# The product of p with its projection computed in the embedding norm's stage, and the gates' two column halves interleaved with a lag of three tiles

## The reference

```python
h = layer_norm(x, ln_emb_g, ln_emb_b)                 # first step of the second block
...
h = layer_norm(DEEPNORM_ALPHA * h + out, ln1_g[i], ln1_b[i])
gate = jax.nn.sigmoid(jnp.einsum('bld,de->ble', h, w_ple_gate[i]))   # 1024 x 1024 weights
ple = jnp.einsum('blq,qd->bld', p[i], w_ple_proj[i])                 # 256 x 1024 weights
h = layer_norm(DEEPNORM_ALPHA * h + gate * ple, ln2_g[i], ln2_b[i])
```

## Time and profile before

| | |
|---|---|
| median of 3 timed runs | 2349.52 us (2346.97 to 2352.33) |
| the profiled execution's own time | 2353.53 us |
| its span in the trace | 2351.8 us |
| TensorE (PE) busy | 2130.5 us, 91% of the span |
| TensorE weight loads (PEld) busy | 1665.2 us, 71% |
| VectorE (DVE) busy | 1750.1 us, 74% |
| ScalarE (ACT) busy | 1057.5 us, 45% |
| GpSimd (POOL) busy | 181.9 us, 8% |
| mean granted TensorE clock | 0.94 |

### The profile page before, as it was taken

The page is one execution under the profiler, slowest core; times in us unless marked ns, Lnnn a source line. Parts: engine busy times, 40 slices in busy tenths (PEclk is TensorE's granted clock), DMA queues, the critical chain, the costliest instruction groups (busy, mean ns, idle before and its releaser), DMA issues. The chain is left out here.

```text
span 2351.8 us, 25583 instructions
## 1 busy us (share of the span) xinstructions
PE 2130.5 (91%) x10156; PEld 1665.2 (71%) x10156; DVE 1750.1 (74%) x1852; ACT 1057.5 (45%) x1194; POOL 181.9 (8%) x154
## 2 busy tenths in 40 slices
PE   5999988999946999999999289999999959899997
PEld 3767835668825888888887168888887647788775
DVE  4575158995575999999997649999999458954727
ACT  4387135773315777777775122221221346622123
POOL 2000010000000111111110200000000010141210
PEclk8999997999967999999999589999999968899999
DMA  9111170002286999999997501212222130332201
GB/s 322 45 36 36 36 283 1 1 1 82 114 315 241 335 395 402 394 394 402 393 394 246 163 13 63 82 36 72 72 99 81 63 117 1 126 116 90 72 1 72
DMA packets 123456, 365.03 MB, mean 155 GB/s; under 512 B 10035, under 2 KB 20683, under 8 KB 123360
## 3 DMA queue, kind: packets, MB, share of 16 engines
q1 hardware_dynamic: 110560, 326.84, 36.4%
q0 software_dynamic: 7568, 23.09, 4.0%
q10 hardware_dynamic: 5232, 13.78, 1.5%
HBM read 324.76 MB, written 38.86 MB: 155 GB/s over the span
## 5 line engine op out<-in xcount | busy, mean ns | idle before, releaser
L2121 DVE SCALAR_TENSOR_TENSOR arena<-arena,vecs 128x1023 f32<-128x1023 f32 (+14 forms) x240 | 304.4, 1268 | 7.1
L1639 DVE TENSOR_TENSOR w_low<-W,w_high 128x2048 fp32r<-128x2048 f32 x96 | 217.0, 2287 | 39.1 <-ACT w_high L1591 39.1
L2018 PE MATMUL Q<-hT_high,w_high 128*128 128x512 f32 (+1 forms) x736 | 227.2, 392 | 5.9 <-DVE ring_low L2164 5.8
L1639 DVE TENSOR_TENSOR w_low<-arena,w_high 128x2048 fp32r<-128x2048 f32 x96 | 218.4, 2290 | 17.7 <-ACT w_high L1591 17.7
L1591 ACT ACTIVATE w_high<-W 128x2048 fp32r<-128x2048 f32 x96 | 184.0, 1919 | 97.0 <-PE Q L1534 65.4
L2018 PE MATMUL Q<-hT_low,w_high 128*128 128x512 f32 (+1 forms) x720 | 222.7, 391 | 0.0
L1591 ACT ACTIVATE w_high<-arena 128x2048 fp32r<-128x2048 f32 x96 | 184.2, 1919 | 74.9 <-PE Q L1534 74.9
L2018 PE MATMUL Q<-hT_high,ring_low 128*128 128x512 f32 x704 | 217.2, 390 | 0.0
L2018 PEld LDWEIGHTS Q<-hT_high,w_high 128*128 128x128 f32 (+1 forms) x736 | 135.5, 184 | 38.9 <-DVE ring_low L2164 5.9
L1534 PE MATMUL Q<-w_high,x_high 128*128 128x512 f32 x512 | 160.8, 396 | 2.4 <-DVE x_low L1642 2.4
L1534 PE MATMUL Q<-w_low,x_high 128*128 128x512 f32 x512 | 158.9, 392 | 0.0
(11 more groups left out here) (450 smaller groups left out, 4304.0 us busy)
## 6 DMA issues: line engine op xcount, KB each, us to landing
W<-in_w_dram SPq DMA_DIRECT2D x48, 2048.0 KB, 12.3
arena<-in_w_dram SPq DMA_DIRECT2D x48, 2048.0 KB, 11.3
W<-in_w_mod_dram SPq DMA_DIRECT2D x12, 2048.0 KB, 13.4
W<-in_w_in_dram SPq DMA_DIRECT2D x12, 2048.0 KB, 8.5
W<-in_w_out_dram SPq DMA_DIRECT2D x6, 2048.0 KB, 11.5
spill<-arena ACTq DMA_DIRECT2D x24, 512.0 KB, 2.6
W<-in_w_in_dram SPq DMA_DIRECT2D x8, 1024.0 KB, 7.2
arena<-in_x_dram SPq DMA_DIRECT2D x4, 1024.0 KB, 17.4
```

The source lines that it names most:

```text
L1639: nc.vector.tensor_tensor(wl[:], chunk_src(r, j), wh[:].bitcast(F32), ALU.subtract).then_inc(low_v, 1)
L2018: ins = nc.tensor.matmul(Q[rows, 2 * (n % 4) + half, :], w[:, k], x[:, k, HALF * half:HALF * half + HALF], start=k == 0 and w is high and ...
L2121: ins = nc.vector.scalar_tensor_tensor(conf[:, i, j:], u[:, 0:S - j], w, conf[:, i, j:], ALU.mult, ALU.add)
```

## The change

The product of p with its projection leaves the tail. In the stage of the embedding norm ScalarE's queue now also loads p and w_ple_proj, TensorE turns p and computes the 16 products (2 before tile 0's transposes, then 2 behind each tile's), ScalarE copies each out of PSUM (`keep_ple`) and stores it to a new DRAM tensor `ple_rows`. In the tail SyncE loads these rows back into `arena`, and VectorE multiplies from there. The gates run in a new order `g_order`: first-half tile q, then second-half tile q - 3.

```diff
+        ple_stage = tiles(12, PLE_SLOTS, HALF)
...
                 act.dma_start(emb_b, bc_row(A["ln_emb_b_2"], D)).then_inc(vec_in, 16)
+                act.dma_start(p_sb, A["p_2"][0, 0].rearrange("(t p) q -> p t q", p=P)).then_inc(p_in, 16)
+                act.dma_start(w_ple, A["w_ple_proj_2"][0].rearrange("(k p) n -> p k n", p=P)).then_inc(w_ple_in, 16)
...
+                def keep_ple(i):
+                    t, n = divmod(i, 2)
+                    j = i % PLE_SLOTS
+                    act.wait_ge(ple_mm, i + 1)
+                    if i >= PLE_SLOTS:
+                        act.wait_ge(ple_stored[j], 16)
+                    nc.scalar.activation(ple_stage[:, j], Q[:, 6 + i % 2, :], ACT.Copy).then_inc(ple_kept, 1)
+                    act.wait_ge(ple_kept, i + 1)
+                    act.dma_start(ple_rows[P * t:P * t + P, HALF * n:HALF * n + HALF], ple_stage[:, j])\
+                        .then_inc(ple_stored[j], 16)
+
                 root(0)
+                act.wait_ge(p_tr, 1)
+                for j in range(2):
+                    nc.scalar.activation(pT[:, j], bank2(2 + j), ACT.Copy).then_inc(pT_ready, 1)
                 for t in range(NT):
                     if t + 1 < NT:
                         root(t + 1)
...
+                    for i in (2 * t, 2 * t + 1):
+                        keep_ple(i)
+                for j in range(PLE_SLOTS):
+                    act.wait_ge(ple_stored[j], 16 * (2 * NT // PLE_SLOTS))
 
             @block.tensor
             def _(pe):
+                def ple(i):
+                    t, n = divmod(i, 2)
+                    if i >= 2:
+                        pe.wait_ge(ple_kept, i - 1)
+                    for k in range(2):
+                        ins = nc.tensor.matmul(Q[:, 6 + i % 2, :], pT[:, k, P * t:P * t + P],
+                                               w_ple[:, k, HALF * n:HALF * n + HALF], start=k == 0, stop=k == 1)
+                    ins.then_inc(ple_mm, 1)
+
+                pe.wait_ge(p_in, 16)
+                for j in range(2):
+                    for t in range(NT):
+                        ins = nc.tensor.transpose(Q[:, 4 + 2 * j + t // 4, P * (t % 4):P * (t % 4) + P],
+                                                  p_sb[:, t, P * j:P * j + P], ident[:])
+                ins.then_inc(p_tr, 1)
+                pe.wait_ge(w_ple_in, 16)
+                pe.wait_ge(pT_ready, 2)
+                ple(0)
+                ple(1)
                 for t in range(NT):
                     pe.wait_ge(emb_ready, t + 1)
...
                     ins.then_inc(emb_tr, 1)
+                    if t + 1 < NT:
+                        ple(2 * t + 2)
+                        ple(2 * t + 3)
...
+        GATE_LAG = 3
+        g_order = [(n, t) for q in range(NT + GATE_LAG) for n, t in ((0, q), (1, q - GATE_LAG)) if 0 <= t < NT]
...
-                sync.dma_start(p_sb, A["p_2"][0, 0].rearrange("(t p) q -> p t q", p=P)).then_inc(p_in, 16)
-                sync.dma_start(w_ple, A["w_ple_proj_2"][0].rearrange("(k p) n -> p k n", p=P)).then_inc(tail_in, 16)
+                sync.dma_start(tiles(8, NT, HALF), ple_of[:, :, 0:HALF]).then_inc(ple_in[0], 16)
+                sync.dma_start(tiles(12, 4, HALF), ple_of[:, 0:4, HALF:]).then_inc(ple_in[1], 16)
...
+                sync.wait_ge(ple_read, g_order.index((0, 3)) + 1)
+                sync.dma_start(tiles(8, 4, HALF), ple_of[:, 4:NT, HALF:]).then_inc(ple_in[2], 16)
...
-                for i in range(2 * NT):
-                    if i == 2:
-                        act.wait_ge(p_tr, 1)
-                        for j in range(2):
-                            nc.scalar.activation(pT[:, j], bank2(j), ACT.Copy).then_inc(pT_ready, 1)
-                    if i == NT // 2:
+                for i, (n, t) in enumerate(g_order):
+                    if (n, t) == (0, 1):
                         unit_high_part(5)
...
-                    if i > NT:
-                        root_2(act, i - NT - 1)
+                    if n == 1 and t:
+                        root_2(act, t - 1)
...
-                        nc.vector.tensor_tensor(g, g, Q[:, i % 4, :], ALU.mult).then_inc(ple_mult, 1)
+                    nc.vector.tensor_tensor(g, g, ple_at[NT * n + t], ALU.mult).then_inc(ple_mult, 1)
```

More of the change, by code:

```diff
@@ L63, in program @@
     cs_rows = dram("cs_rows", (P, P))
+    ple_rows = dram("ple_rows", (S, D))
     def cols(w, c0, n=HALF):
@@ L1759, in program @@
         emb_T_low = sem("emb_T_low")
+        p_sb = tiles(32, NT, 256)
+        w_ple = tiles(34, 2)
+        pT = tiles(36, 2)
+        PLE_SLOTS = 8
+        ple_stage = tiles(12, PLE_SLOTS, HALF)
+        p_in, w_ple_in, p_tr, pT_ready = sem("p_in"), sem("w_ple_in"), sem("p_tr"), sem("pT_ready")
+        ple_mm, ple_kept = sem("ple_mm"), sem("ple_kept")
+        ple_stored = [sem(f"ple_stored{j}") for j in range(PLE_SLOTS)]
         emb_stored = sem("emb_stored")
@@ L2471, in program @@
         b_out, ln1_g, ln1_b = tiles(32), tiles(33), tiles(32)
-        p_sb = tiles(8, NT, 256)
-        pT = tiles(10, 2)
-        w_ple = tiles(12, 2)
+        ple_at = [tiles(8, 12, HALF)[:, (NT * n + t) % 12] for n in range(2) for t in range(NT)]
         ln2_g, ln2_b = tiles(14), tiles(15)
@@ L2478, in program @@
         res_in = [sem(f"res_in{j}") for j in range(2)]
-        rows_in, p_in, tail_in = sem("rows_in"), sem("p_in"), sem("tail_in")
+        rows_in, tail_in = sem("rows_in"), sem("tail_in")
+        ple_in = [sem(f"ple_in{j}") for j in range(3)]
         res_scaled, ln1_b_in = sem("res_scaled"), sem("ln1_b_in")
@@ L2504, in program @@
         for n in range(2):
-            used_at[U_PLE + n] = (gate_mm, NT * (n + 1))
+            used_at[U_PLE + n] = (gate_mm, g_order.index((n, NT - 1)) + 1)
         def tile_cols(t):
@@ L2611, in gate @@
                     product(4 + n, t, 4 + i % 4, h1T_high, h1T_low).then_inc(gate_mm, 1)
[L2613 to L2618, removed]
-                                               w_ple[:, k, HALF * n:HALF * n + HALF], start=k == 0, stop=k == 1)
-                    ins.then_inc(ple_mm, 1)
-                for i in range(4):
-                    gate(i)
                     if i < len(LATE):
                         turn_h1(LATE[i])
-                pe.wait_ge(p_in, 16)
-                pe.wait_ge(h1T_low_ready, NT)
-                for j in range(2):
-                    for t in range(NT):
-                        ins = nc.tensor.transpose(Q[:, 2 * j + t // 4, P * (t % 4):P * (t % 4) + P],
-                                                  p_sb[:, t, P * j:P * j + P], ident[:])
-                ins.then_inc(p_tr, 1)
-                gate(4)
-                pe.wait_ge(tail_in, 48)
-                pe.wait_ge(pT_ready, 2)
-                for i in range(4):
-                    ple(i)
-                for i in range(4, 2 * NT):
-                    if i > 4:
-                        gate(i)
-                    ple(i)
             @block.scalar
```

33 lines of the change are left out of this document (15 added, 18 removed).

## The result

The changed kernel takes 2371.32 us (median of 4 runs, 2368.73 to 2372.50) against 2348.46 for the kernel before (4 runs on the same chip, 2346.97 to 2352.33): ratio 1.0093, 95% interval 1.0079 to 1.0106. It is 22.9 us slower; +19.3 was predicted. The profiled execution took 2368.73 us, the lowest of its four, and that of before 2353.53, above all four of its own, so the two traces stand only 15.2 apart. The stages are therefore compared by lengths within each trace.

What follows compares the result with a forecast made beforehand. TensorE was taken to bound the tail, VectorE's pace the norm's stage. Tail -19.0 and stage +38.3 summed to +19.3 us, on a median of 2349.5 giving 2369 us, range 2351 to 2391.

Steps and rivals of the forecast that it cites:

- (1): Tail: p's transposes and products 0 to 14 leave TensorE before the last gate ends, -27.5 us.
- (3): Tail: gates come in pairs of 11 us; VectorE's 9.5 us after a gate fit in, costing nothing.
- the tail gives less: Rival, tail: late roots reach back to TensorE through sigmoids, tail loses up to 8 us, 2377 us; no separate chance.
- (2): Tail: fifth gate waits for GpSimd's remainders of the second half's weights, needed sooner, +4.8 us (0 to 7).
- (4): Tail's end: last three gates are second-half, VectorE falls behind, last pass 15.1 us after last gate, +3.7 us.
- (5): Norm's stage: p lands late, at 1331 (1324 to 1335); its transposes and copies then run to 1336.6.
- (6): Norm's stage: products 0 and 1 take 5.7 us ahead of tile 0, which with late p starts +22.3 us later.
- (7): Norm's stage: a loop of TensorE and ScalarE sets 6.8 us per tile at clock 0.87, +13.2 us.
- half clock all through: Rival, norm's stage: clock stays at 0.50, periods of 10.5 us, net +46, 2396 us; chance 0.12.
- (8): Norm's stage's end: last copy, products and wait for the last store take 5.8 us, +2.8 us.
- full clock and an early p: Rival, norm's stage: p by 1324 and every period 6.2 us, net +6, 2355 us; chance 0.14.
- The other side: Rival, both places: p in by 1317, stage +17.8, tail gives 23.8, net -6, 2343 us; chance 0.06.

Runs made afterwards that it cites:

- lag8: Changed kernel with the second-half gates eight tiles behind the first instead of three, so all first-half gates come first: 2366.09 us, ratio to before 1.0071.
- poollate: Changed kernel with GpSimd's small loads in the norm's stage held until p and its weight have landed: 2357.68 us, ratio to before 1.0032.
- keepfirst: Changed kernel with ScalarE copying and storing the product's two half tiles before the tile's transposes instead of after: 2363.41 us, ratio to before 1.0055.
- early: Changed kernel with p and its weight loaded by SyncE behind the experts' last weights: 2341.24 us, ratio to before 0.9968.
- best: Changed kernel with the edits of early and keepfirst, a four-tile gate lag, and p's copies ahead of ScalarE's first root: 2325.24 us, ratio to before 0.9893.

## Why the prediction was nearly right

Sign, size and both places were right; that the size came so near is partly luck, since the misses of single steps cancel. By steps:

(1) and (3) held. -27.5 was what left TensorE, and VectorE's waits for the late roots never reached back to TensorE: behind the fifth gate it has no wait, and a pair of gates takes 10.88. (The gates themselves took 5.44 instead of 5.49, another 0.5 in all.) So the rival "the tail gives less" falls.

(2), +4.8 for the fifth gate, was 1.6 too small. Without the wait the fifth gate would have ended at 2281.5, 5.44 behind the fourth, and it ended at 2288.0, +6.4. ScalarE and GpSimd began as put (0.49 and 1.19 behind the first sigmoid's start), but the eight remainders took 12.72 instead of 11.23. The runs give it independently: with lag 8 the tail is 5.2 shorter although its end is 1.3 longer, 6.5 together.

(4), +3.7, measured +4.3 (15.7 behind the last gate; 15.1 was put). The reason given, second-half gates in a row, where VectorE needs 6.37 and TensorE 5.44, and a VectorE that enters them behind, fits the chain: it leaves TensorE at gate 13, and from there to the last pass it is 32.1 us, where the working has 31.5 (2297.8 to 2329.3). In lag8, with eight in a row, the end is longer still. Tail: -27.5 - 0.5 + 6.4 + 4.3 = -17.3 instead of -19.0.

(5) is the step that failed, in size and partly in reason. p was put at 1331, 24.6 us behind ScalarE's first issue; it came at 32.2 behind it, 7.6 later and outside the bounds. I took the slow stretch as given and had p share it with the tokens, but let it land before the last of them; it came behind them (the last tile landed 26.3 us after its issue at 1308.9, so at 1335.2). What made the stretch wasn't asked. poollate shows that it is GpSimd's small loads: without them p comes 11.7 us sooner.

(6) was +22.3 and came out at +29.4 with p's lateness; from p's landing to tile 0's transposes it was 1347.88 - 1337.04 = 10.8 us, where 11.3 was put.

(7) was +13.2 and came out at +8.9. The ring was right (keepfirst), the clock too low. I took 0.87 from the state-space stage; it was 1.00 throughout, and the period 6.18, the 6.2 given for full clock. So the rival "half clock all through" falls. The Trainium skill's rule in "TensorE: Matmul & The Clock Gate", Part 4, that transposes don't count as busy for the clock, isn't tested by the trace of after, where full clock came with products, but early, poollate and best speak against it: there p's transposes alone brought the clock from 0.50 to 1.00, before any product. For this case the measurement decides. Why the 64 transposes of before stayed at 0.50 stays open.

(8) was +2.8. From tile 7's transposes to the next stage's first product it was 9.18 us before and 9.96 after, +0.8: the stores land sooner than the 2.6 taken for them (2.0 from issue to landing in the median), and the transposes themselves are 0.93 shorter at full clock, which I had not counted. That the last store ends the stage is borne out by keepfirst, where it is issued sooner and the next stage's first product waits 6.47 us instead of 8.05.

(6) with p's lateness missed by +7.1, (7) by -4.3 and (8) by -2.0, so that the stage's +38.3 stands against 39.05: the sum is better than its parts, and this is the luck in it.

Of the rivals, "full clock and an early p" was half right, in its clock. The other side was right as a mechanism: early brings the stage's growth down to 10.7 us, less than the tail's 17.3, and is faster than before by 7.5.

## What to carry to other kernels

Work moved under another engine's cover has to have its inputs there: 2 MB issued at the moment of use cost 28 of the 39 us, and issued a block ahead nothing to be seen. Before a load is put into a slow stretch of the DMA engines, ask what makes it slow; here 0.25 MB of small loads, wanted much later, slowed what was left of 7 MB. In a ring of two engines empty the bank that the other one waits for first, and leave enough independent work between asking for a slow engine's result and needing it (here one tile more of lag).

## What the runs showed of the hardware

- GpSimd's small loads slowed every queue: 126 GB/s at a DMA share of 0.77 (after), against 402 at 1.03 with them moved away (poollate). Share and rate together show it: the engines are busy with little to move.
- Of VectorE's seven SBUF passes that begin beside GpSimd's remainders in after, six take 1.64 to 1.76 us instead of 0.69, two multiplies among them (the third took 0.79); in before the multiplies beside GpSimd, with their operand in PSUM, took 0.69. And GpSimd's eight take 9.99 us with VectorE idle, 11.23 in the kernel before, 12.72 to 12.83 in the changed ones.
- TensorE's clock rose during p's products in after, but during p's transposes alone in early, poollate and best. In after it stayed at 1.00 in a loop that left it idle for a quarter of the time (35.79 of 47 us busy). In best, a gap of 2.99 us behind the first products came with half-clock transposes; the gaps of 1.60 in every period of early did not. A gap isn't the whole of it: in best the clock had been at 0.50 from 1309.5 to 1312.5 too, while TensorE worked on the products without one.
